# Where TensorE spreads the next token's query in a decode step on one core

## What is computed

```
k_past = cache_fox_k[l, page_table]        # 8 requests x 16 pages x 128 tokens x 8 heads x 128
s_past = einsum('bthd,bshd->bhts', q, k_past) * scale + cq + tail
p = softmax(concatenate([s_past, s_new]))
out = einsum('bhts,bshd->bthd', p[..., :P], v_past) + ...
```

## Time and profile before

| | |
|---|---|
| median of 3 runs | 1632.56 us (1632.38 to 1638.49) |
| the profiled execution | 1634.03 us, its span 1632.3 us |
| busy in the span | PE 93%, PEld 86%, DVE 63%, ACT 38%, POOL 14% |
| granted TensorE clock, mean | 0.97 |
| turns 0 to 8 | from about 78 us to about 650 us of the span |

### The profile page before, as it was taken

How to read it: one execution, slowest core, us unless ns; L and a number is a source line. 1 busy time by engine, 2 the same in 40 slices (tenths; PEclk the granted TensorE clock), 3 DMA queues, 4 the chain that set the end, 5 groups by cost and what they waited for, 6 DMA issues and landing times.

```text
span 1632.3 us, 32704 instructions
## 1 busy us (share of the span) xinstructions
PE 1516.0 (93%) x12249; PEld 1402.8 (86%) x12249; DVE 1030.0 (63%) x3226; ACT 613.1 (38%) x721; POOL 235.2 (14%) x331
## 2 busy tenths in 40 slices
PE   4999987799898899999889999999999999999996
PEld 4999865577776677998689999999999999999996
DVE  4589899998976776567375555544445555554444
ACT  3342232232234452444453333333333333333443
POOL 3011222222222123330230000000000000000221
PEclk9999989999999999999699999999999999999998
DMA  8558999999998799553345555544555555554553
GB/s 322 175 190 304 398 364 412 408 382 381 376 386 312 256 390 392 204 184 129 107 153 181 180 180 180 180 148 159 180 191 197 180 180 180 180 180 136 182 177 124
DMA packets 78979, 388.42 MB, mean 238 GB/s; under 512 B 9096, under 2 KB 9872, under 8 KB 56864
## 3 DMA queue, kind: packets, MB, share of 16 engines
q1 hardware_dynamic: 35424, 230.90, 39.5%
q0 software_dynamic: 39376, 143.15, 23.2%
q10 hardware_dynamic: 4080, 13.12, 2.0%
HBM read 377.03 MB, written 10.10 MB: 237 GB/s over the span
## 4 chain that ended last, share of the span: by engine, by line
PE 73%; DVE 15%; DMA 5%; ACT 4%; issue 3%; ACTq 0%; DVEq 0%; SPq 0%; POOLq 0%; POOL 0%
PE bank L1541 22%; PE bank L1542 21%; PE bank L1543 21%; DVE page L1082 5%; DVE wlo L1026 3%; DMA page<-kc_dram 2%; PE bank L1698 2%; ACT whi L601 1%; DVE wlo L991 1%; DMA raw<-p_out_dram 1%; ACT whi L564 1%; DMA raw<-p_in_dram 1%; DMA page<-vc_dram 1%; PE bank L1894 0%; PE bank L1620 0%
## 5 line engine op out<-in xcount | busy, mean ns | idle before, releaser
L1541 PE MATMUL bank<-hh,whi 128*128 128x264 f32 (+1 forms) x2368 | 693.9, 293 | 36.1 <-DVE wlo L1026 23.1
L1542 PE MATMUL bank<-hl,whi 128*128 128x264 f32 (+1 forms) x2368 | 677.3, 286 | 0.0
L1543 PE MATMUL bank<-hh,wlo 128*128 128x264 f32 (+1 forms) x2368 | 676.6, 286 | 0.0
L991 DVE TENSOR_TENSOR wlo<-raw,whi 128x2048 fp32r<-128x2048 f32 (+1 forms) x174 | 357.9, 2057 | 276.7 <-ACT whi L564 276.7
L1541 PEld LDWEIGHTS bank<-hh,whi 128*128 128x128 f32 x2368 | 452.6, 191 | 73.3 <-issue 41.9
L564 ACT ACTIVATE whi<-raw 128x2048 fp32r<-128x2048 f32 (+1 forms) x174 | 299.3, 1720 | 532.9 <-PE bank L1543 525.3
L1542 PEld LDWEIGHTS bank<-hl,whi 128*128 128x128 f32 x2368 | 453.3, 191 | 0.6 <-issue 0.2
L1543 PEld LDWEIGHTS bank<-hh,wlo 128*128 128x128 f32 x2368 | 451.1, 190 | 0.0
L1082 DVE CUSTOM_DVE_ANT_0 page<-page,qb 128x128 f32<-128x128 f32 x1024 | 226.1, 283 | 15.7 <-ACT qb L646 11.3
L1541 PE MATMUL bank<-f_hi,whi 128*128 128x264 f32 x704 | 201.9, 287 | 7.5 <-DVE f_lo L1513 7.5
L1543 PE MATMUL bank<-f_hi,wlo 128*128 128x264 f32 x704 | 201.4, 286 | 0.0
(11 more groups left out here) (296 smaller groups left out, 1430.3 us busy)
## 6 DMA issues: line engine op xcount, KB each, us to landing
raw<-p_gu_dram SPq DMA_DIRECT2D x88, 1024.0 KB, 4.9
page<-kc_dram POOLq DMA_DIRECT2D x128, 512.0 KB, 8.2
page<-vc_dram POOLq DMA_DIRECT2D x128, 512.0 KB, 8.3
raw<-p_in_dram SPq DMA_DIRECT2D x48, 1024.0 KB, 8.4
raw<-p_dn_dram SPq DMA_DIRECT2D x64, 704.0 KB, 4.1
raw<-p_out_dram SPq DMA_DIRECT2D x16, 1024.0 KB, 5.4
raw<-p_mem_dram SPq DMA_DIRECT2D x8, 1024.0 KB, 7.3
x_res<-x_fm_dram SPq DMA_DIRECT2D x8, 528.0 KB, 10.3
```

Of the source, the lines that this page charges most:

```text
L991: tt(wlo[:, (k + 2) % 4, 0:blocks * P], raw[:, (k + 2) % 4, 0:blocks * P], whi[:, k % 2, 0:blocks * P], ALU.subtract).then_inc(S("w_split" ...
L1541: mm(out, blk(whi, k % 2, b), rh, start=start, stop=False)
L1542: mm(out, blk(whi, k % 2, b), rl, start=False, stop=False)
L1543: return mm(out, blk(wlo, k, b), rh, start=False, stop=stop)
```

## The change

`q_spread` moves within PE's stream and `select` within DVE's. A table gives the part of each of the turns 0 to 6. PE now spreads as the first piece of that part, ahead of its quarters, and DVE selects as the last thing of the part before. PE's spread also gets a wait for ACT's last copy of `qb` out of banks 2 and 3; in turn 6 it keeps its wait for `a_olo`. ACT's stream is as it was: `q_copy` stays in part 15.

```
+SPREAD_AT = (12, 12, 15, 15, 12, 12, 15)
...
-                if t <= 6 and j == (15 if t in (2, 3) else 12):
+                if t <= 6 and j == SPREAD_AT[t] - 1:
                     select(t + 1, query_select(t + 1))
...
             for g in range(16 * TURNS):
                 t, j = g // 16, g % 16
+                if t <= 6 and j == SPREAD_AT[t]:
+                    pe.wait_ge(S("q_b"), 2 * t + 2)
+                    if t == 6:
+                        pe.wait_ge(S("a_olo"), 4)
+                    q_spread(t + 1)
                 for n, (p, q) in enumerate(quarters(t, j)):
...
-                if t <= 6 and j == 15:
-                    if t == 6:
-                        pe.wait_ge(S("a_olo"), 4)
-                    q_spread(t + 1)
```

## The result

| | before | with the change |
|---|---|---|
| median of 6 runs each, taken together | 1634.03 us (1632.38 to 1638.49) | 1647.09 us (1643.66 to 1651.15) |
| ratio, 95% interval | 1 | 1.0077 [1.0062, 1.0092] |
| profiled execution, its span | 1634.03, 1632.3 us | 1646.29, 1644.6 us |

The change makes the kernel 13 us slower. The forecast was 1637.4 us in a range of 1629 to 1643: the sign of the sum was right, its size was not.

A forecast was written before the change was run, and what follows sets the result against it. The prediction took PE to bound the kernel overall, with DVE and page loads pacing some turns. Its terms 4.0 - 1.2 - 1.6 - 1.8 + 5.4 = +4.8 us gave 1637.4 us, range 1629 to 1643.

The forecast's parts named there:

- turn 0, +4.0: Turn 0, part 12: PE waits 3.4 us for the selection, low clock adds 1.6, two `wlo` waits return 1.0: +4.0 us.
- the 1.6 us for the low clock: Turn 0, behind the new wait: 3.5 us mostly at 1.2 instead of 2.4 GHz cost 1.6 us more.
- end of turn 1, -1.2: End of turn 1: selection early enough, DVE regains 1.9 us, but the panel comes 0.7 us later: -1.2 us.
- ends of turns 2 and 3, -1.6: Part 15: PE waits 2.3 us for the selection and gains little; DVE regains 0.80 and 0.8 us: -1.6 us.
- turns 4 and 5, -1.8: Part 12 waits of 0.6 and 2.1 us; 3.0 us come back, 1.9 lost again, 0.7 saved: -1.8 us for both.
- 2.1 + 0.7 - 0.9 = 1.9 of the 3.0 are lost again: Turn 5, part 12: wait 2.1 us plus spread 0.7, less DVE's 0.9 in hand, loses 1.9 of 3.0 us returned.
- turn 6, +5.4: Turn 6, part 15: PE waits 5.4 us, delaying panel 47, panel 49's load and the head of turn 7: +5.4 us.
- a slower load: Turn 6, load of panel 49: upper bound of that term, +6.5 us instead of +5.4.
- PE pays and gets nothing back: Rival, turns 4 and 5: stalls become waits for panels; +11.0 us, 1643.6 us, if over 3.4 us of gains fail; chance 0.17.
- DVE's stalls come back in full: Rival: in turns 2 and 5 DVE is the fullest engine; sum -2.6 us, 1630 us; chance 0.13.
- The load has slack: Rival, turn 6: panel 49's load has slack or the selection comes sooner; sum -0.6 us, 1632 us; chance 0.17.
- selections in time: Rival, all places: new waits do not form and all DVE stalls return; -12.5 us, 1620 us; chance 0.03.

The follow-up runs named there:

- selearly: The change with its spread places kept, but DVE selecting in parts 10, 8, 9, 8 and 12 of turns 0, 1, 4, 5, 6: 1630.94 us, 0.9982 of before.
- sel6: Kernel before with only turn 6's spread moved to the head of part 15, selection in part 12 as before: 1634.73 us, 1.0007 of before.
- only0: Kernel before with the change's new places in turn 0 alone: 1641.15 us, 1.0045 of before.
- warm0: The change in turn 0 alone, plus 28 matmuls with unread results ahead of the spread, filling PE's wait: 1638.69 us, 1.003 of before.
- only145: Kernel before with the change's new places in turns 1, 4 and 5 alone: 1634.89 us, 1.0013 of before.
- only6: Kernel before with the change's new place in turn 6 alone: 1641.03 us, 1.0048 of before.
- warm6: The change in turn 6 alone, plus 46 filler matmuls ahead of the spread: 1643.77 us, 1.0061 of before.
- late45: Kernel before with only turns 4 and 5 changed: spread at the head of part 14, selection in part 12 as before: 1628.72 us, 0.9973 of before.
- only23: Kernel before with the change's new places in turns 2 and 3 alone: 1637.04 us, 1.002 of before.
- end23: Kernel before with only the selection of turns 2 and 3 moved from part 15 to 14, spreads at the turns' ends: 1634.66 us, 1.0003 of before.
- best: Against before: spread at head of part 14 in turns 0, 1, 4, 5, turn ends elsewhere; selection in part 14 in turns 2 and 3: 1628.82 us, 0.9965.
- best2: Like the run best, but turns 4, 5, 6 spread in parts 12, 12, 15 with selections in parts 9, 8, 12: 1626.15 us, 0.9955 of before.

## Why the prediction was wrong

**Right: the waits and their places.** PE's six waits were forecast at 3.4, 2.3, 2.3, 0.6, 2.1 and 5.4 us, 16 in all, and are 3.3, 2.8, 2.6, 0.7, 2.2 and 5.9, 17.5 in all. DVE's waits for `qb` fell to 0.5 us (forecast: under 2). The spread of turn 0 starts at 135.91 (forecast 135.6). The load chain of turn 6 is the one described, and selearly and sel6 show that the late selection causes it.

**Wrong: turn 0, +4.0.** It is +5.1. The failed step is the 1.6 us for the low clock. I took one stretch of 3.5 us from turn 3, where PE is not the limit, as its length. only0 against warm0 gives 3.0 us, and the granted clock in only0 is 0.50 not for 3.5 but for 6.8 us, from 137.9 to 144.7:

```profile
137.90:144.70 6.80, 6.80 (x29) 6.15 (x29) 3.09 (x30) 0.00 (x0) 1.06 (x2) 0.50 0.65 219
```

By the Trainium skill's rule (TensorE: Matmul & The Clock Gate, HAM oscillation), half of the throttled time is lost; for 6.8 us that is an estimate of 3.4 us, near the 3.0 measured. So the rule agrees roughly, and the length that I put into it did not. That PE's waits for `wlo` in turn 1 would go and return 1 us was near: from the head of turn 1 to part 6 it is +6.7 to +5.4, 1.3 us. With that the terms close: 3.3 + 3.0 - 1.3 = 5.0.

**Right: end of turn 1, -1.2.** DVE goes from +5.4 in turn 1 to +4.2 us in turn 2, and only145 and selearly show the same 1.2.

**Not settled: ends of turns 2 and 3, -1.6.** The trace has +4.1 us, but most of that is not the change's. From part 4 of turn 2 to part 3 of turn 4 seven kernels with before's order there also fall behind its profiled execution: only6 by 5.4 us (+0.2 to +5.5), only145 4.1, warm0 4.0, sel6 4.0, warm6 3.5, only0 2.9 and late45 0.5. With before itself at 0 their mean is 3.0. The three with the change's order there have 4.1 (the change), 3.3 (selearly) and 2.4 (only23), in the mean 3.3. That shows no gain of 1.6 us, and no loss that stands out from the scatter. The execution profiled before was lucky there. It was unlucky later: the granted clock from 650 to 882 us is 0.92 in it and 0.95 in the change's, and between turn 8 and 882 us only6 and sel6 come nearer again by 3.7 and 3.1 us, the change by 5.7 from turn 7 on. only23 by itself gives +0.2% with an interval that holds zero.

**Wrong: turns 4 and 5, -1.8.** Nothing is returned: from part 11 of turn 4 to part 14 of turn 6 the change stays at +8.3 us, only145 goes from +2.0 to +2.3, and its time stands at 1.0013. The failed step is in part 12 of turn 5, "2.1 + 0.7 - 0.9 = 1.9 of the 3.0 are lost again": it holds no low clock, though I had put one behind the wait of turn 0. Busy time of the stretch behind the spread, with the change:

```profile
442.00:447.40 5.40, 5.40 (x30) 4.84 (x34) 1.61 (x17) 0.07 (x1) 0.53 (x1) 0.68 1.03 416
```

At 0.68 the 24 matmuls take 4.7 us (442.56 to the value page at 447.22), not 2.9. With 1.8 us for that, 2.2 + 0.7 + 1.8 - 0.9 = 3.8 us, which is DVE's wait of 3.79 at 447.33 to 0.1 us. So the 3.6 us that PE had won by part 6 were lost in full. That the low clock is what was missing shows in only145: the same wait of 2.23 us in turn 5 is followed there by a clock of 1.00, and turn 5 keeps 2.1 us, near the -3.0 + 1.9 - 0.7 = -1.8 of my terms. But there the clock falls behind the wait of turn 4, where the trace loses 2.4 us. Why it falls behind one wait in one trace and behind the other in the other, no run shows. late45 shows that the gain is there (-0.27%) once PE does not wait.

**Wrong: turn 6, +5.4.** It is 8.6 us alone and 9.9 in the change. The failed step is the landing time of the load of panel 49: it took 7.1 us (7.8 in only6), not 5.4. I took its time from the earlier trace rows for a load that goes out at another moment, beside other page loads. I had "a slower load" as a bound, but priced it at 1.1 us. The wait was also 0.5 us longer. (The term has a slip too: 527.9 + 5.4 is 533.3 and not 533.5, which makes it 5.2.) With 1.7 us for the load and 0.5 for the wait, 5.2 becomes 7.4; PE is 7.8 us later at the head of turn 7 (+8.3 to +16.1). The last 2.1 us come from there to part 4 of turn 7. Other traces move by -1.4 to +1.2 us in that stretch, and the clock of the change is low in parts of it (0.67 from 547 to 555 us); what part of it belongs to the change is not shown.

**The rivals.** "PE pays and gets nothing back" was the nearest. Of the 4.6 us of gains only the 1.2 of turn 1 are seen for certain, so 3.4 failed if the unsettled 1.6 are counted with them, which is just its point of decision. Its mechanism, stalls for the query that turn into waits for panels, is what turn 5 shows. Its price of +11.0 us was short of 13, since it used the same 4.0 and 5.4. "DVE's stalls come back in full", 1630 us, did not come about. The rule that I set beside it, to optimize the most contended engine first (the Trainium skill, Perfetto Trace Analysis, Identifying the Most-Contended Engine), did not help here, where relieving DVE in turn 5 (57 of 62 us busy) held PE; late45, which relieves DVE without holding PE, bears it out in part. "The load has slack" and "selections in time" are refuted by only6 and by the waits of the change. The range ended at 1643 because I bounded what follows a wait of PE place by place; but the time at low clock and the time of the load came out high in turns 0, 5 and 6 together.

## What to carry to other kernels

Before a consumer is moved forward on the engine that bounds, look at each new place whether its input is there, and move the producer first: the same places cost 13 us with late selections and gain about 3 us with early ones (in all turns but 2 and 3), at the edge of what 12 runs can tell. A wait on the bounding engine costs its length and, where they follow, the low clock behind it and the lateness of the load that its next step releases; here 9.2 us of waits in turns 0 and 6 cost 14 to 15. To compare two traces step by step, have several kernels with no difference in that stretch: over turns 2 and 3 such traces lay up to 5.4 us apart by chance, over the end of turn 0 less than 0.1.

## What the runs showed of the hardware

The low clock behind a short wait is not certain. At the end of turn 3 the kernel before waits 1.74 us for the selection, only6, with the same instructions there, 1.54 us. From 330 to 336 us, of before and of only6:

```profile
330.00:336.00 6.00, 6.00 (x53) 4.41 (x52) 5.92 (x42) 0.89 (x3) 2.64 (x5) 1.00 1.03 411
```

```profile
330.00:336.00 6.00, 6.00 (x26) 5.37 (x25) 3.68 (x33) 3.16 (x7) 1.58 (x3) 0.50 1.03 414
```

53 matmuls start in one and 26 in the other. Seven executions have such a wait of 1.5 to 1.8 us there: before and late45 stay at 1.00 behind it, only0 is at 0.50 for 3.4 us, and only6, only145, sel6 and warm6 for 6.8 to 6.9 us. end23, best and best2, which have no wait there, stay at 1.00. The low clock also comes without a wait for the selection: in warm0 it had fallen 4 us ahead of this place, and before is at 0.50 from 524 to 534 us. This fits runs of one kernel that lie up to 11 us apart (1628.28 to 1639.55 in one set), and the runs bear it out in part: in that set the five fastest of 30 had a mean granted clock of 0.971 to 0.974, the five slowest 0.964 to 0.970.

The load of panel 49, 1 MB on the same queue, took 4.8 to 5.4 us to land in the eleven traces without a late selection in turn 6 (5.4 before, 4.9 in sel6), and 7.1 (the change), 7.3 (warm6) and 7.8 us (only6) in the three with one. While it was on its way 0.1 MB of page loads moved beside it before and in sel6, and 1.2 to 1.3 MB in the change, warm6 and only6. That these make it slow is my reading; no run took them away. A chain through such a load should carry 5 to 8 us.
